# Projections that start on x times the norm's weight, with the norm's scale applied to each chunk after the matmuls

## The reference

```python
def rmsnorm(x, g):
    xf = x.astype(jnp.float32)
    y = xf * lax.rsqrt(jnp.mean(xf * xf, axis=-1, keepdims=True) + EPS)
    return (y * g.astype(jnp.float32)).astype(x.dtype)

def conv_ffn(h, w_up, conv_w, conv_b, w_down):     # 1024 -> 5632 -> (gate, val) 2816 each -> 1024
    u = h @ w_up
    u = conv over 3 tokens, each feature by itself, causal (u, conv_w) + conv_b
    gate, val = jnp.split(u, 2, axis=-1)
    return (jax.nn.silu(gate) * val) @ w_down

for i in range(2):
    h = rmsnorm(x, norm_mix[i])
    x = x + (even_mixer(h, ...) if i == 0 else odd_mixer(h, ...))
    x = x + conv_ffn(rmsnorm(x, norm_ffn[i]), ...)
```

## Time and profile before

| | |
|---|---|
| three runs, us | 1462.26, 1462.53, 1467.37 |
| the profiled execution's own time, us | 1466.21 |
| its span in the profile, us | 1464.4 |
| PE busy (matmuls) | 1392.3 us, 95% |
| DVE busy | 872.1 us, 60% |
| ACT busy | 802.6 us, 55% |
| POOL busy | 547.2 us, 37% |
| chain that ended last | PE 87%, DVE 6%, ACT 3%, POOL 2%, issue 2% |
| norm 1, FFN 0 up chunks, norm 2, norm 3 at | 152, 158 to 290, 359, 524 us |

### The profile page before, as it was taken

How to read it: one execution, slowest core, us unless ns; L and a number is a source line. 1 busy time by engine, 2 the same in 40 slices (tenths; PEclk the granted TensorE clock), 3 DMA queues, 4 the chain that set the end, 5 groups by cost and what they waited for, 6 DMA issues and landing times.

```text
span 1464.4 us, 25774 instructions
## 1 busy us (share of the span) xinstructions
PE 1392.3 (95%) x11032; PEld 1347.1 (92%) x11032; DVE 872.1 (60%) x1047; ACT 802.6 (55%) x954; POOL 547.2 (37%) x249
## 2 busy tenths in 40 slices
PE   6999899998999979999999998999999999899997
PEld 5989899998999979999988997999988998899996
DVE  4865666755555467666759767434445876734443
ACT  4655577765676457777536544454324554455431
POOL 5000288885331337988606000564000600066300
PEclk9999999999899989999999999999999999999998
DMA  7433677777654466777624444555542543355550
GB/s 261 142 115 115 222 275 261 256 292 305 224 207 159 140 239 241 264 262 269 229 103 170 169 145 144 178 191 179 192 150 80 199 155 144 137 192 190 177 198 29
DMA packets 40002, 278.22 MB, mean 190 GB/s; under 512 B 4432, under 2 KB 4560, under 8 KB 8144
## 3 DMA queue, kind: packets, MB, share of 16 engines
q1 hardware_dynamic: 32976, 226.23, 43.8%
q10 hardware_dynamic: 6912, 50.33, 8.9%
HBM read 275.50 MB, written 1.05 MB: 189 GB/s over the span
## 4 chain that ended last, share of the span: by engine, by line
PE 87%; DVE 6%; ACT 3%; POOL 2%; issue 2%; DMA 0%; DVEq 0%; ACTq 0%; SPq 0%; POOLq 0%
PE bank L738 22%; PE bank L740 22%; PE bank L739 22%; PE bank L703 3%; PE bank L704 2%; PE bank L710 2%; DVE low L1421 2%; PE bank L952 1%; PE bank L722 1%; PE bank L724 1%; PE bank L723 1%; PE bank L772 1%; PE bank L759 1%; DVE h L1554 1%; ACT high L1068 1%
## 5 line engine op out<-in xcount | busy, mean ns | idle before, releaser
L1421 DVE TENSOR_TENSOR low<-raw,high 128x2048 fp32r<-128x2048 f32 (+4 forms) x222 | 510.8, 2304 | 306.0 <-ACT high L1068 303.7
L738 PE MATMUL bank<-op_high,low 128*128 128x256 f32 x1904 | 549.1, 288 | 3.3 <-DVE low L1421 3.3
L739 PE MATMUL bank<-op_low,high 128*128 128x256 f32 x1904 | 540.5, 284 | 0.0
L740 PE MATMUL bank<-op_high,high 128*128 128x256 f32 x1904 | 540.4, 284 | 0.0
L1068 ACT ACTIVATE high<-raw 128x2048 fp32r<-128x2048 f32 (+4 forms) x222 | 406.3, 1831 | 155.2 <-PE bank L740 143.6
L738 PEld LDWEIGHTS bank<-op_high,low 128*128 128x128 f32 x1904 | 367.4, 193 | 8.8 <-DVE low L1421 4.4
L739 PEld LDWEIGHTS bank<-op_low,high 128*128 128x128 f32 x1904 | 367.3, 193 | 2.8 <-issue 2.4
L740 PEld LDWEIGHTS bank<-op_high,high 128*128 128x128 f32 x1904 | 367.1, 193 | 0.0
L738 PE MATMUL bank<-act_high,low 128*128 128x256 f32 x864 | 242.7, 281 | 0.0
L740 PE MATMUL bank<-act_high,high 128*128 128x256 f32 x864 | 242.0, 280 | 0.0
L739 PE MATMUL bank<-act_low,high 128*128 128x256 f32 x864 | 240.6, 278 | 0.0
(11 more groups left out here) (288 smaller groups left out, 1910.6 us busy)
## 6 DMA issues: line engine op xcount, KB each, us to landing
raw<-stream SPq DMA_DIRECT2D x198, 1024.0 KB, 4.8
adaw<-ada ACTq DMA_DIRECT2D x48, 1024.0 KB, 6.2
raw<-stream SPq DMA_DIRECT2D x10, 768.0 KB, 4.5
raw<-stream SPq DMA_DIRECT2D x10, 512.0 KB, 3.6
x<-xT SPq DMA_DIRECT2D x1, 1024.0 KB, 5.1
out<-h SPq DMA_DIRECT2D x1, 1024.0 KB, 3.9
raw<-stream SPq DMA_DIRECT2D x2, 384.0 KB, 3.3
consts<-consts_d SPq DMA_DIRECT2D x1, 672.0 KB, 14.1
```

The lines of the kernel that those rows point to most:

```text
L738: pe.matmul(o, wl[:, w], oh[:, k, :], start=one, stop=False, skip_group_check=True)
L739: pe.matmul(o, wh[:, w], ol[:, k, :], start=False, stop=False, skip_group_check=True)
L740: mm = pe.matmul(o, wh[:, w], oh[:, k, :], start=False, stop=end, skip_group_check=True)
L1421: dve.tensor_tensor(low[m % SPLIT][:, 0:w], raw[m % RAW][:, 0:w], high[m % SPLIT][:, 0:w], ALU.subtract).then_inc(S["low_ready"], 1)
```

## The change

Norms 0 to 3 no longer stand ahead of their projection. A stage `xg` splits x * g, without rstd, pair by pair as x gets ready. The first two chunks of each mixer, and all 22 up chunks of each FFN, multiply that; they are called DEFERRED. When such a chunk is done, DVE multiplies the bank by `rn` into SBUF (`scaled_to`: quarters of `h`, or a buffer `Sb`), which frees the bank, and everything that read the bank reads that copy. In the mixers the other chunks still multiply a normed and split h, which is now formed beside the first two chunks. The convolution of an up chunk is issued behind the scaling of the chunk after it, `gate` and `val` have three buffers, and the act stage of j-1 is issued with the v chunk. The sum of the last squares stands in the middle of the first chunk. At the start of the program `ar` and `la` come behind `bk0` and `bv0`, the first two units' sums stand next to each other, and SP loads the constants behind the first weight chunk and most parameters behind the second. In the diff the first `xg` is ACT's and the second DVE's, and the last three pieces are DVE's.

```diff
-RAW, SPLIT, RELU = 3, 3, 3
+RAW, SPLIT, RELU, CONV = 3, 3, 3, 3
...
+        FIRST = {"bq0": 0, "up0g0": 1, "od000": 2, "up1g0": 3}
+        DEFERRED = {"bq0": 0, "bk0": 0, "od000": 2, "od001": 2}
+        DEFERRED.update({f"up{l}{v}{j}": 2 * l + 1 for l in range(2) for v in "gv" for j in range(11)})
+        def scaled_to(name):
+            if name in ("bq0", "bk0"):
+                return Sb[name == "bq0"][:]
+            at = 2 * (int(name[4]) if name.startswith("od") else (2 * int(name[4:]) + (name[3] == "v")) % 4)
+            return h[:, at:at + 2, :]
...
                     st_("square", (i, pair)), st_("square_add", (i, pair))
+                    if i in XG_HIGH:
+                        st_("xg", (i, pair))
...
-        st_("trig"), st_("norm", 0), st_("ar")
-        c("bq0"), st_("la")
-        c("bk0", split=False), st_("unit", 0), st_("la_exps"), high_low("bk0")
-        c("bv0", split=False), st_("unit", 1), st_("lam"), high_low("bv0")
+        st_("first_split"), st_("norm", 0), c("bq0"), c("bk0", split=False), st_("ar"), high_low("bk0")
+        c("bv0", split=False), st_("unit", 0), st_("unit", 1), st_("la"), high_low("bv0"), st_("la_exps"), st_("lam")
...
-                    c(f"up{l}{half}{j}")
-                    if half == "g" and j:
-                        st_("act", (l, j - 1))
+                    c(name, split=False)
+                    if taken is not None:
+                        st_("conv", taken)
+                    high_low(name), st_("conv_init", name)
                     if half == "v":
+                        if j:
+                            st_("act", (l, j - 1))
                         st_("silu", (l, j))
+                    taken = name
                     modulation()
-            st_("act", (l, 10))
+            st_("conv", taken), st_("act", (l, 10))
...
+            if name in DEFERRED:
+                return S["first_scaled"], SCALED[name] + 1
...
+                        if name in FIRST and at == 4:
+                            if name == "bq0":
+                                sumsq((0, 2))
+                            sumsq((FIRST[name], 3))
...
+            def xg(a):
...
+                for k in (2 * p, 2 * p + 1):
+                    ins = act.activation(XG_HIGH[i][:, k, :], x[:, k, :], ACT.Copy, scale=gains[i][:, k:k + 1])
...
+            def xg(a):
...
+                for k in (2 * p, 2 * p + 1):
+                    ins = dve.scalar_tensor_tensor(out=XG_LOW[i][:, k, :], in0=x[:, k, :], scalar=gains[i][:, k:k + 1],
+                                                   in1=XG_HIGH[i][:, k, :], op0=ALU.mult, op1=ALU.subtract)
...
+                if name in DEFERRED:
+                    dve.wait_ge(S["rstd_ready"], DEFERRED[name] + 1)
+                    dve.wait_ge(S["products_done"], n + 1)
+                    dve.tensor_tensor(scaled_to(name), ps[b][:], rn[:].rearrange("p (a b) -> p a b", a=1)
+                                      .to_broadcast([P, 2, TOK]), ALU.mult).then_inc(S["first_scaled"], 1)
...
-                            ins = dve.scalar_tensor_tensor(out=dst[:, i, d:], in0=ps[b][:, i, 0:TOK - d],
...
+            def conv(name):
...
+                dst, src = (cg, cv)[v][j % CONV], scaled_to(name)
...
+                        ins = dve.scalar_tensor_tensor(out=dst[:, i, d:], in0=src[:, i, 0:TOK - d],
                                                            scalar=col("conv", t + tap, 1), in1=dst[:, i, d:],
                                                            op0=ALU.mult, op1=ALU.add)
```

More of the change, by code:

```diff
@@ L277, in build @@
         AL = f("act_low", [P, 22, TOK], F32R)
-        cg = [f(f"gate{i}", [P, 2, TOK]) for i in range(2)]
-        cv = [f(f"val{i}", [P, 2, TOK]) for i in range(2)]
+        cg = [f(f"gate{i}", [P, 2, TOK]) for i in range(CONV)]
+        cv = [f(f"val{i}", [P, 2, TOK]) for i in range(CONV)]
         ffn.close()
@@ L390, in projection @@
             for n, name in enumerate(names):
-                c(name)
+                final = i in XG_HIGH and n + 1 == len(names)
+                c(name, split=not final)
                 if pair > behind:
@@ L534, in build @@
                 done = BY[i]["n"]
-            elif stage == "norm" and i:
+            elif stage == "norm" and i not in XG_HIGH:
                 BEFORE_NORM[i] = done
@@ L642, in operand_wait @@
                     return S["operand_low"], lambda k: FILLS["mix0"] + MIX_ORDER.index(k) // 2 + 1
-                if name in ("up0g0", "up1g0"):
-                    return S["operand_low"], lambda k: FILLS["n1" if name[2] == "0" else "n3"] + k // 2 + 1
-                if name == "od000":
+                if name == "od010":
                     return S["operand_low"], lambda k: FILLS["n2"] + k // 2 + 1
@@ L758, in sumsq @@
                 for k in (2 * p, 2 * p + 1):
-                    mm = pe.matmul(ps[NB][:, 0, :], col("ones"), h[:, k, :], start=not i and k == 0, stop=k == KB - 1)
+                    mm = pe.matmul(ps[NB][:, 0, :], col("ones"), h[:, k, :], start=False, stop=k == KB - 1)
                 if p == 3:
@@ L1385, in gla_o @@
                 act.wait_ge(S["gla_o_done"], hp + 1)
[L1386 removed]
+                squares_of(GLA_U[hp], ps[UNIT_AT[GLA_U[hp]]][:])
             def diff_n(i):
                 act.wait_ge(S["diff_pv"], 4 * i + 4)
[L1390 to L1392 removed]
+                squares_of(DIFF_U[i], ps[OB][:])
+            stages = dict(chunk=chunk, conv_init=conv_init, high=high_after, xg=xg, first_split=first_split, square=square, norm=norm, late=late, dil_o=dil_o, mla_p=mla_p, unit=unit,
                           turns=turns, lam=lam, ar=ar_, la=la_, la_exps=la_exps, ket=ket,
@@ L1609, in unit @@
                         r = slice(64 * half, 64 * half + 64)
-                        ins = dve.scalar_tensor_tensor(out=(Qd, Kd)[k][:, half, 2 * hp:2 * hp + 2, :],
-                                                       in0=ps[bank_of(BY[("bq0", "bk0", "bq1", "bk1")[u]])][r],
+                        name = ("bq0", "bk0", "bq1", "bk1")[u]
+                        src = scaled_to(name) if name in DEFERRED else ps[bank_of(BY[name])]
+                        ins = dve.scalar_tensor_tensor(out=(Qd, Kd)[k][:, half, 2 * hp:2 * hp + 2, :], in0=src[r],
                                                        scalar=col(("dq_gain", "dk_gain")[k])[r], in1=rb[u % 2][r],
@@ L1806, in mla_p @@
                         .then_inc(S["att_low"], 1)
-            stages = dict(chunk=chunk, low=low_after, square_add=square_add, norm=norm, late=late, unit=unit, lam=lam, la=la_, la_exps=la_exps, gla_att=gla_att,
+            stages = dict(chunk=chunk, conv=conv, low=low_after, xg=xg, first_split=first_split, square_add=square_add, norm=norm, late=late, unit=unit, lam=lam, la=la_, la_exps=la_exps, gla_att=gla_att,
                           gla_kv=gla_kv, gated=gated, mix=mix, diff_s=diff_s, diff_w=diff_w, dil_s=dil_s,
```

200 lines of the change are left out of this document (125 added, 75 removed).

## The result

The changed kernel takes 1506.02 us (median, 1504.77 to 1510.95) where the kernel before, run beside it, takes 1464.61 us (1462.26 to 1467.37): a ratio of 1.0292, 95% interval 1.0263 to 1.0321. It is slower by 41.4 us. The prediction said 1516 us and slower; the time lies in its range of 1462 to 1558. The profiled execution took 1505.87 us.

The account below looks back on a forecast made before the run. PE was taken to set the time inside the stages, with the norms as gaps. Norms -14.5, start +4 and FFNs +66 gave +55 us: 1517 against the median of 1462.53, stated as 1516, range 1462 to 1558.

Parts of the forecast that it names:

- Norms, -14.5: Norms 1, 2 and 3: PE's gaps shrink, saving 6.3, 5.6 and 2.6 us, together 14.5 us.
- the new wait for the head sum: Norm 2: PE's sum between `od001` and `od010` waits for DVE's late scaling, giving back 2.5 us of 8.1.
- Start, +4: Program start: `bq0` earlier, but sums, `ar`, `la` and softmax delay the first mixer; 4 us lost, bounds -2 and +8.
- The 3 us wait for the softmax: First mixer: gates' logarithms and scans ahead of the softmax make W late, so PE waits 3 us more.
- FFNs, +66: Both FFNs: convolution reading SBUF and POOL's instructions exclude each other; 66 us lost, from 35 to 100.
- the excess of 64: Up chunks: mutually exclusive DVE and POOL instructions exceed PE's time by 34 us in FFN 0 and 30 in FFN 1.
- the third rival: FFN stalls: the same loss with PE at its lower level in them, above 1560 us; chance 0.06.
- a reserve (-12): Up chunks: low ends before PE takes its chunk, so 6 us per FFN come off the loss.
- idle port (+8): FFNs: times when neither DVE nor POOL holds the port, 0 to 15 us per FFN, taken as 4.
- act_low (+6): Third down chunk: act_low of j=10 comes later behind its convolution, making PE wait 3 us per FFN.
- The first (no exclusion, 1458): FFN convolution from SBUF runs beside POOL if DVE's waits stay under some 1.5 us a pair: 1458 us; chance 0.14.
- The second (POOL pays): FFNs: exclusion holds, but POOL falls behind and catches up in the down chunks; about 15 us each, 1482 us; chance 0.12.

Follow-up runs that it names:

- bank_and_later_sums: Changed kernel, up chunks' scaling written back into the PSUM bank the convolution reads, five modulation sums one chunk later: 1455.15 us, 0.9923 of the kernel before.
- bank_sums_table: bank_and_later_sums with the adaLN step of the last up chunk moved out of the up stage by the table, sums of segments 2 and 10 one chunk later: 1464.51 us.
- all_mended: bank_and_later_sums with last up chunk's modulation step behind act_low, two head sums behind `od010`, first head sum at the start moved up: 1472.27 us.
- the start alone: bank_and_later_sums with only the first chunk's head sum moved up behind the decay product: 1452.52 us, 0.9905 of the kernel before.
- both edits together: bank_and_later_sums with the table edit of bank_sums_table and the moved head sum of the start alone: 1463.71 us, 0.9979 of the kernel before.

## Why the prediction was right, and where it was off

**Norms, -14.5: right.** Norm 1 saved 6.65 us (152.37 to 163.01 before, 151.35 to 155.34 now, from its sum to the third group of `up0g0`) against 6.3. Norm 2 saved 8.3 against 8.1 up to the fourth group; the new wait for the head sum is 2.35 us against 2.5, but `od010` behind it took 7.56 us, 1.4 more than before, which I had not counted. Norm 3 saved 4.0 against 2.6, though its wait grew from 5.43 to 6.63 us.

**Start, +4: too high.** `bq0` started at 15.34 (16.5 said), `bq1` at 44.73 (46), `aq` at 62.33 against 60.33 before: +2.0. The 3 us wait for the softmax did not come; W ended at 60.02, ahead of the transposes at 60.40. That step of the prediction failed: the gates' work on ACT and DVE (45 to 53 us) ran while PE was in `bq1` (44.73 to 52.25). By the end of the mixer PE was 1.0 us ahead of before, but not through the new start: the stretch from 100 to 128 us ran at a clock of 0.88 in the trace of the kernel before (162 matmuls) and of 1.00 in that of the changed kernel (187). That clock also differs between kernels that are alike up to there (last section). Where it was 0.94 with either start, the sum of norm 1 stood at 151.66 us with the old one and at 152.07 and 152.13 with the new, so the new start costs 0.4 to 2 us.

The version with the bank and the later sums (1455.15) shows what is left of the change without its fault: 11.0 us gained, where -14.5 + 4 is 10.5. The sum is near for other reasons, though. By its profile it gains 1.0 us up to norm 1, 6.5 and 5.9 in the up chunks with the norm ahead of them and 1.3 in the second mixer, and loses 5.1 in the down chunks of FFN 0, where it waits 2.98 us for act_low and runs on at a lower clock.

**FFNs, +66: right in cause, too large, and made of other parts.** Measured: 29.7 and 26.6 us, 56.3 in all. The cause, DVE's convolution and POOL's additions shutting each other out, is shown by the table of experiments. Up chunks of FFN 0 took 151 us from their first matmul; from 155 to 165 were said. My working added up the time of every instruction with two SBUF inputs on DVE and of every one on POOL, as if PE had to wait for the whole excess. But the eight convolution instructions of a pair don't all meet POOL: the value chunk's are at 0.48 to 0.50 us, only the gate chunk's are caught. So the excess of 64 was nearly twice the stalls, 33.4 us of idle time. What brought the total near is a term I left at nothing, slower matmuls after the stalls: 22.8 us. I had named them only in the upper bound and in the third rival. That the two errors nearly cancel is luck: with the stalls sized right and no term for the clock, the forecast would have been some 33 us lower, under the 1490 of its own range. The waits were not where I had put them either: I named low, and act_low with 6 us, but PE waited 11.4 us for low, 9.9 for act_low and 12.8 for the additions ahead of modulation sums, which my sum does not hold. The terms for a reserve (-12), idle port (+8) and act_low (+6) can't be read apart; act_low alone waited 7.50 and 2.43 us. The runs split the loss otherwise: 34.5 us go with the convolution's source, 16.3 more with late sums. (The terms sum to 1517; the 1516 stated is 1 us off its own sum.)

**The rivals.** The first (no exclusion, 1458) is what the kernel does once the source is the bank and the sums are later: 1455.15. Its condition was the right one, though with the source alone put right it is 1471. The second (POOL pays) did not hold: DVE's gate convolution was held up, and POOL's busy time fell. In the up chunks of FFN 0 POOL's second addition has a mean of 2441 ns (L1933), no longer the 4423 of the earlier trace rows; but its first is now at 3524 (L1932), where it was at 2417, so each side holds up the other. Of the third, the lower clock was real, but as a part of the loss, not on top of it.

## What to carry to other kernels

Before an operand moves from PSUM to SBUF, list what the other engine on that memory runs at the same moment: in this kernel the move cost 30 us beside long additions and 3.5 without them. Price a PE stall with what the clock takes behind it: five waits of 6.8 us in all cost 17.4 us of their stages. And where an engine is near its limit, a wait removed elsewhere pays only once that engine is in time; the same edit gave 16.3 us in one kernel and nothing in the other.

## What the runs showed of the hardware

A DVE instruction with two SBUF inputs was held up by one long POOL instruction after the other: four that take 1.78 us undisturbed took 6.39 us (at 262.40) and, at the next pair's place, 7.34 us. With a PSUM input the same four took 1.77 us beside the same additions. A stall of PE of 1.38 us was followed by a granted clock of 0.71 over the next 5.7 us, and without the stall the same stage ran at 1.00; one of 3.10 us was followed by 0.50, the 1.2 GHz level, over the next 6 us. And the clock can differ where the program does not. The start and the first mixer of bank_sums_table are those of bank_and_later_sums, instruction for instruction, yet in the one profiled execution of the table's kernel the mixer ended 3.6 us later (155.0 against 151.4). The stretches from 44 to 62 and from 100 to 128 us, first of bank_and_later_sums, then of bank_sums_table:

```profile
44.00:62.00 18.00, 18.00 (x121) 0.91 0.30 112
...
100.00:128.00 28.00, 26.58 (x187) 1.00 0.23 76
```
```profile
44.00:62.00 18.00, 18.00 (x113) 0.82 0.29 106
...
100.00:128.00 28.00, 26.58 (x168) 0.89 0.23 78
```

The other traces show the same. Seven kernels have this start and first mixer: in four traces the stretch from 100 to 128 us was at 1.00 and the mixer ended at 151.35 to 151.52 us, in two at 0.94 (152.07 and 152.13), in one at 0.89 (155.00). all_mended, the start alone and both edits together share the other start: with the first head sum moved the first scores of all_mended began 4.0 us earlier than its base's, and the mixer ended 0.5 us later, behind 100 to 128 us at 0.88; with the start alone that stretch was at 1.00 and the mixer ended 2.0 us earlier, with both it was at 0.94 and 0.5 us earlier. The kernel before, too, has runs from 1461.98 to 1468.29 us, the shortest nine at a mean clock of 0.977, those over 1467.5 us at 0.972 or 0.973. So of the 9 us of bank_sums_table 3.6 may be of this kind, and differences of under 5 us between two kernels should not be read from one execution each. What decides the clock there stays open; no run here was made for it.
